# Prompt values of the expert layer by a dense pass over the value table, and another order of the row requests in the sample steps

## The reference

```
qh  = (xc @ wq) ...;  s = einsum(qh, sub_keys)          # 8 heads, two halves of 128 keys
sv, si = top_k(s, 16); cand = sv0[:, None] + sv1[None, :]; fv, fi = top_k(cand, 16)
eidx = si0 * 128 + si1 at fi;   g = softmax(fv)
act = gelu(einsum("td,trkd->trk", xc, u_tab[eidx]))
out = einsum("trk,trkd->td", g * act, v_tab[eidx])
h = h + out;   y = h + sigmoid(rmsnorm(h) @ w_gate) * (p @ w_ple)
```

## Time and profile before

| | |
|---|---|
| runs | 2516.59, 2518.28, 2526.69 us |
| profiled execution, span | 2524.0 us, 21534 instructions |
| PE busy | 1685.6 us (67%) |
| DVE busy | 1161.0 us (46%) |
| POOL busy | 913.2 us (36%) |
| ACT busy | 320.3 us (13%) |
| bytes moved by DMA | 908.75 MB, mean 360 GB/s |

### The profile page before, as it was taken

One profiled execution on the slowest core, in us unless ns is written; L12 is line 12 of the kernel. 1 busy time (PEld: TensorE's weight loads), 2 busy tenths in 40 slices (PEclk: granted clock), 3 DMA queues, 4 the chain that ended last, 5 costly groups with the idle time before them and its releaser, 6 DMA issues.

```text
span 2524.0 us, 21534 instructions
## 1 busy us (share of the span) xinstructions
PE 1685.6 (67%) x8372; PEld 917.0 (36%) x8372; DVE 1161.0 (46%) x2146; ACT 320.3 (13%) x705; POOL 913.2 (36%) x644
## 2 busy tenths in 40 slices
PE   8999989997997649688788332233333223577778
PEld 3445665696775337433376000000000000122224
DVE  2010322134455763544533666565565765644433
ACT  0000221010002322200200100101001012101002
POOL 0000000012234443422533556565666665645440
PEclk9998997998998776599699666656666665778799
DMA  9943483779999997999999999999999999999998
GB/s 358 333 164 123 125 315 107 268 254 411 366 399 375 369 379 301 391 382 373 400 411 360 418 418 422 421 421 421 422 421 421 421 421 418 402 416 416 416 415 325
DMA packets 215844, 908.75 MB, mean 360 GB/s; under 512 B 17350, under 2 KB 40879, under 8 KB 131808
## 3 DMA queue, kind: packets, MB, share of 16 engines
q0 software_dynamic: 92160, 671.13, 64.4%
q1 hardware_dynamic: 123126, 235.36, 26.3%
q10 hardware_dynamic: 458, 0.91, 0.1%
HBM read 895.31 MB, written 14.53 MB: 360 GB/s over the span
## 4 chain that ended last, share of the span: by engine, by line
DMA 48%; PE 40%; DVE 4%; POOL 3%; issue 3%; ACT 2%; SPq 0%; ACTq 0%; DVEq 0%; PEldq 0%; POOLq 0%
DMA arena<-in_peer_v,arena 31%; PE bank L1747 9%; PE bank L2182 5%; DMA arena<-in_w_in 5%; PE bank L2197 5%; DMA arena<-in_peer_u,arena 4%; DMA arena<-in_peer_wq 3%; DMA arena<-in_w_out 3%; PE bank L1821 3%; PE bank L1958 2%; PE bank L1934 2%; PE bank L2306 2%; PE bank L2131 2%; POOL arena L669 2%; PE bank L2108 1%
## 5 line engine op out<-in xcount | busy, mean ns | idle before, releaser
L1530 DVE CUSTOM_DVE_ANT_0 arena<-arena 128x2048 f32<-128x2048 f32 x320 | 730.7, 2292 | 581.5 <-DMA arena<-in_peer_u,arena 578.1
L2182 PE MATMUL bank<-arena 128*32 128x512 f32 x2560 | 459.9, 823 | 672.7 <-DVE arena L1539 539.1
L669 POOL DMA_INDIRECT arena<-in_peer_u,arena x320 | 561.2, 1754 | 860.6 <-DVEq L1509 566.4
L674 POOL DMA_INDIRECT arena<-in_peer_v,arena x320 | 351.7, 1099 | 689.6 <-PE bank L2182 663.2
L2182 PEld LDWEIGHTS bank<-arena 128*32 128x32 f32 x2560 | 67.1, 127 | 1003.7 <-DVE arena L1539 522.6
L1747 PE MATMUL bank<-arena 128*128 128x512 f32 (+2 forms) x544 | 216.3, 558 | 5.4 <-PE bank L1747 4.1
L2197 PE MATMUL bank<-arena 128*128 128x192 f32 x1024 | 189.9, 348 | 24.4 <-DMA arena<-in_w_in 23.2
L2197 PEld LDWEIGHTS bank<-arena 128*128 128x128 f32 x1024 | 181.5, 205 | 45.6 <-DMA arena<-in_w_in 28.5
L1747 PEld LDWEIGHTS bank<-arena 128*128 128x128 f32 (+1 forms) x544 | 101.4, 208 | 116.7 <-issue 116.4
L2306 PE MATMUL bank<-arena 128*128 128x512 f32 x256 | 125.6, 650 | 0.0
L986 ACT ACTIVATE arena<-arena 128x4 f32<-128x4 f32 x80 | 16.8, 210 | 849.6 <-DVE arena L1530 849.4
(11 more groups left out here) (270 smaller groups left out, 1490.5 us busy)
## 6 DMA issues: line engine op xcount, KB each, us to landing
arena<-in_w_in SPq DMA_DIRECT2D x22, 2048.0 KB, 9.4
arena<-in_w_in SPq DMA_DIRECT2D x32, 1024.0 KB, 14.6
arena<-in_w_out SPq DMA_DIRECT2D x8, 2048.0 KB, 9.7
arena<-in_peer_wq SPq DMA_DIRECT2D x8, 2048.0 KB, 8.1
arena<-in_w_out SPq DMA_DIRECT2D x16, 1024.0 KB, 16.3
arena<-in_peer_wq SPq DMA_DIRECT2D x16, 1024.0 KB, 23.0
arena<-in_ple_gate SPq DMA_DIRECT2D x32, 512.0 KB, 15.4
arena<-in_ple_gate SPq DMA_DIRECT2D x6, 2048.0 KB, 13.3
```

The source lines that it names most:

```text
L669: pool.indirect_dma_start(u_row[j], None, I["peer_u"][0], bass.IndirectOffsetOnAxis(idx[:, i, c + j:c + j + 1], 0)).then_inc(u_in[j], 16)
L674: pool.indirect_dma_start(v_row[j], None, I["peer_v"][0], bass.IndirectOffsetOnAxis(idx[:, i, c + j:c + j + 1], 0)).then_inc(v_in[j], 16)
L1530: dve.tensor_tensor_reduce(out=u_row[j], in0=u_row[j], in1=rep_of(i), scale=1.0, scalar=0.0, op0=ALU.mult, op1=ALU.add, accum_out=a4[:, pa ...
L2182: ins = pe.matmul(bank[i % 2][32 * q:32 * q + 32, :], diag[:, k % 2, j, :], v_row[j][:, 512 * q:512 * q + 512], start=(s == 0 and j == 0), ...
```

## The change

There are two parts.

For the eight prompt groups no value rows are gathered. After a group's dot products, its weights (32 tokens x 128 picks, one gelu for the whole group) are spread into a table of 128 x 128 experts per token: per step ScalarE builds four one-hot matrices of the first key index (`hot_rows`), VectorE four of the second, scaled by the weight (`hot_columns`), and TensorE multiplies them (`spread_picks`, four 128x128x128 matmuls); ScalarE copies the result (`spread_copy`) and writes it per group to DRAM (2 MB). The batches of a group run in the eight steps of the group behind it, those of the last group all in step 64. Then, in iterations 1 to 10 of the sample steps, TensorE multiplies the weights with the whole value table (134 MB, loaded by SyncE in 128 tiles of 1 MB): 32 `dense_group`s of 32 matmuls, 128x128 weights by 512 columns. VectorE adds each result to `h` (`dense_out`). The prompt's gate moves behind it, to iterations 11 to 14, eight quarters in each.

In the sample steps GpSimd no longer asks for four key tiles and then four value tiles: it asks for value tile j of step k and then key tile j of step k+1. In the prompt steps it asks for key tiles only.

Some semaphores are merged or renamed, and a row of 128 numbers is added to the constants; these edits are left out below.

```diff
+    BATCHES = 8 * DSUBS          # DSUBS = 8
+    GROUPS = 32
+    DENSE0, GATE0 = 1, 11
+    def groups_at(i, j):
+        n, slots = 4 * (i - DENSE0) + j, 4 * (GATE0 - DENSE0)
+        if not 0 <= n < slots:
+            return range(0)
+        return range(n * GROUPS // slots, (n + 1) * GROUPS // slots)
+    def batches_at(k):
+        if k < SSTEP or k > LAST:
+            return range(0)
+        return range(k - SSTEP, k - SSTEP + 1) if k < LAST else range(BATCHES - 8, BATCHES)
     # SyncE
+        def dense_rows(n):
+            c, half, pair = n // 8, n // 4 % 2, n % 4
+            if n >= 4:
+                sp.wait_ge(dense_used, n - 3)
+            j0 = 8 * c + 2 * pair
+            sp.dma_start(dense_v[n % 4], v_rows[:, j0:j0 + 2, 1024 * half:1024 * half + 1024]).then_inc(ring4_in[n % 4], 16)
+        sp.wait_ge(spread_out, 16 * (DSUBS - 1))
+        sp.wait_ge(spread_last, 16)
+        dense_weights(0)
+        for n in range(4 * GROUPS):
+            if n % 8 == 2 and n < 120:
+                dense_weights(n // 8 + 1)
+            dense_rows(n)
     # GpSimd
+        for k in range(LAST + 1):
+            for j in range(4):
+                key_rows(k, j)
+        for k in range(LAST, STEPS):
             for j in range(4):
+                value_rows(k, j)
+                if k + 1 < STEPS:
+                    key_rows(k + 1, j)
     # ScalarE
+        def hot_rows(n):
...
+            for x in range(4):
+                ins = act.activation(rows[:, x, :], key_iota, ACT.Square, scale=-1.0,
+                                     bias=pick_i[:, i % 4, t0 + x:t0 + x + 1])
+            ins.then_inc(squared, 1)
+            act.wait_ge(squared, n + 1)
+            act.activation(rows, rows, ACT.Relu, scale=-1.0, bias=1.0).then_inc(hot_i_ready, 1)
     # VectorE
+            for x in range(4):
+                ins = dve.tensor_scalar(hot_j[place][:, par, x, :], key_iota, pick_j[:, i % 4, t0 + x:t0 + x + 1],
+                                        wT[:, i % 2, t0 + x:t0 + x + 1], ALU.is_equal, ALU.mult)
+            ins.then_inc(hot_j_ready, 1)
+        def behind_dot(i, j):
+            if i == 0 and j == 0:
+                turn_weights(DSUBS - 1)
+                for n in batches_at(LAST):
+                    hot_columns(n)
+            for g in groups_at(i - 1, j):
+                dense_out(g)
     # TensorE
+        def dense_group(g):
+            c, half = divmod(g, 2)
+            if g == 0:
+                pe.wait_ge(spread_ev, BATCHES)
+            if half == 0:
+                pe.wait_ge(dense_set, 2 * c + 2)
+            for pair in range(4):
+                n = 4 * g + pair
+                pe.wait_ge(ring4_in[n % 4], dense_v_count(n))
+                for x in range(4):
+                    t, q = divmod(x, 2)
+                    if pair == 0 and 4 * g + x >= 6:
+                        pe.wait_ge(dense_ev, 4 * g + x - 5)
+                    for j in range(2):
+                        ins = pe.matmul(dense_bank(g, x)[:, :], dense_w[c % 2][:, 2 * pair + j, t].rearrange("p s t -> p (s t)"),
+                                        dense_v[n % 4][:, j, 512 * q:512 * q + 512],
+                                        start=(pair == 0 and j == 0), stop=(pair == 3 and j == 1))
+                    if pair == 3 and x < 3:
+                        ins.then_inc(dense_mm, 1)
+                ins.then_inc(dense_used, 1)
         for i in range(2 * SSTEP):
+            if i == GATE0:
+                h_turns()
...
+            for j in range(4):
+                for g in groups_at(i, j):
+                    dense_group(g)
+                weighted_tile(LAST + i, j)
+                if GATE0 <= i < GATE0 + 4:
+                    for q in range(2):
+                        prompt_gate(8 * (i - GATE0) + 2 * j + q)
```

More of the change, by code:

```diff
@@ L28 @@
 STEPS = SUBS * SSTEP
+DSUBS = 8
 EARLY = 4 * SSTEP
@@ L330, in ring_of, with dense_v_count, gate_count, dense_w_count @@
         return f % 3 if f < 16 else f % 4
+    def dense_v_count(n):
+        return 16 * (sum(ring_of(f) == n % 4 for f in range(32)) + n // 4 + 1)
+    def gate_count(q):
+        if q >= 29:
+            return 16 * 3
+        return 16 * ((11, 11, 10, 0, 0)[q % GW] + q // GW + 1)
+    def dense_w_count(c):
+        return 16 * (2 + c + 1)
     def ring_count(f):
@@ new lines, in spread_copy @@
+        def spread_copy(n):
+            i, t0 = n // 8, 4 * (n % 8)
+            act.wait_ge(spread_mm, n + 1)
+            if n % 8 == 0 and 0 < i < DSUBS - 1:
+                act.wait_ge(spread_out, 16 * i)
+            act.activation(spread[batch_place(n)[0]][:, :, t0:t0 + 4],
+                           batch_bank(n)[:, :].rearrange("p (t j) -> p j t", t=4), ACT.Copy).then_inc(spread_ev, 1)
+            if n % 8 == 7:
+                act.wait_ge(spread_ev, n + 1)
+                act.dma_start(w_dram[i], spread[batch_place(n)[0]].rearrange("p j t -> p (j t)"))                   .then_inc(spread_out if i < DSUBS - 1 else spread_last, 16)
@@ new lines, in step_batches, with dense_turn @@
+        def step_batches(k):
+            for n in batches_at(k):
+                hot_rows(n)
+                if n:
+                    spread_copy(n - 1)
+            if k == LAST:
+                spread_copy(BATCHES - 1)
+        def dense_turn(c):
+            if c >= 2:
+                act.wait_ge(dense_used, 8 * (c - 1))
+            for t in range(2):
+                act.wait_ge(half_in[t], dense_w_count(c))
+                act.activation(dense_w[c % 2][:, :, t], dense_in[t].rearrange("p s j t -> p j s t"), ACT.Copy).then_inc(dense_set, 1)
@@ L996, in acc_out @@
+        def acc_out(i):
+            act.wait_ge(v_used, 4 * SSTEP * (i - DSUBS + 1))
+            if i > DSUBS:
+                act.wait_ge(h_seen, 1)
             r = tile_of(i)[1]
@@ L1093, in _ @@
                     spread_rows(SUBS - 1, g)
-            if s == SSTEP - 1:
+            if k < LAST:
+                step_batches(k)
+            if k == LAST:
+                dense_turn(0)
+                dense_turn(1)
+            if k >= LAST and s == SSTEP - 1:
                 acc_out(k // SSTEP)
@@ L1506, in pick @@
             else:
+                if i < DSUBS:
+                    for turned, e in ((pick_i, e0), (pick_j, e1)):
+                        ins = dve.transpose(turned[:, i % 4, :], e.rearrange("p a b -> p (a b)"))
+                    step(ins)
                 step(dve.scalar_tensor_tensor(out=e0, in0=e0, scalar=float(NKEY), in1=e1, op0=ALU.mult, op1=ALU.add))
@@ L1662, in _ @@
                 spread_staged(i + 1)
-            if s == 0 and k:
+            if s == 0 and i > DSUBS:
                 add_peer(i - 1)
+            if s == 0 and 0 < i < DSUBS:
+                turn_weights(i - 1)
+            if k < LAST:
+                for n in batches_at(k):
+                    hot_columns(n)
             if k in late:
@@ L2242, in _, with spread_picks @@
             late_quarter(0, q)
+        def spread_picks(n):
+            place, par = batch_place(n)
+            pe.wait_ge(hot_i_ready, n + 1)
+            pe.wait_ge(hot_j_ready, n + 1)
+            if n >= 2:
+                pe.wait_ge(spread_ev, n - 1)
+            for x in range(4):
+                ins = pe.matmul(batch_bank(n)[:, NKEY * x:NKEY * x + NKEY], hot_i[place][:, par, x, :], hot_j[place][:, par, x, :],
+                                start=True, stop=True)
+            ins.then_inc(spread_mm, 1)
         for k in range(EARLY):
```

327 lines of the change are left out of this document (189 added, 138 removed).

## The result

The changed kernel takes 2993.55 us (median of four runs, 2984.87 to 2997.2) against 2519.61 us (the median with a fourth run): the ratio is 1.187, with a 95% interval of 1.184 to 1.191. The forecast was 2920 us, a ratio of 1.16, and a range of 2830 to 3050. The direction and the main mechanism were right.

A forecast was written before the change was run, and what follows sets the result against it. DMA bytes were taken to bound most of the kernel, with TensorE idle time. From step 0 at 560 us, 638 + 465 + 41 + 975 + 198 + 40 gave about 2920 us; range 2830 to 3050.

The forecast's parts named there:

- What bounds the kernel, and where the pass stands: Bytes are scarce and TensorE has idle time, but the dense pass stands behind step 64, none in steps 28 to 63.
- The pass, 975 us: Iterations 1 to 10: 1024 matmuls at 0.873 us, 894; tiles 45, group boundaries 20, empty slots and clock dips 16.
- Steps 0 to 27, 638 us: Now 824 us, less 132.8 of value tiles' TensorE work and 53.0 of idle time; ends 521 and 752.
- I let these be paid by the waits that shrink: Steps 0 to 27: added picks (TensorE 24 us) and batch work cost nothing net, as waits shrink with DMA load.
- keep their chain: Rival, 12%: in the first 28 steps one wait takes another's place, 752 us instead of 638, 3035 in all.
- Steps 28 to 63, 465 us: Now 732 us; VectorE takes over from DMA at 12.75 us a step, 459, plus 6 for short steps.
- The lock rival: Rival, 8%: in prompt steps each dot also waits for GpSimd's issue, 16.4 us a step, 3045 in all.
- Step 64, 41 us: Step 64 until the pass: batches 22, last copy 1, write 7, weight load back 4, turning and dot 0; ends 25, 60.
- The order of the requests, 0 us: Sample steps: GpSimd's alternating value and key tiles move nothing, at most a tile's 6 us of landing.
- The rival on bytes: Rival, 3%: 100 MB less moved decides, 2473 us at 0.437 us a dense matmul; gain below 0.486.
- The signs: Step 28 near 1200, step 64 near 1660, 12 to 13 us a step between, VectorE above 90% busy, DMA near 0.8.
- the three signs of being wrong: A dense matmul under 0.8 us, TensorE waiting for table tiles, or steps 28 to 63 at 15 us or more.

The follow-up runs named there:

- experiments 3 to 5: Changed kernel with half the dense matmuls left out, with only the first four table tiles loaded, and with both: 2637.8, 2993.2 and 2555.0 us.
- 6: Changed kernel with 12 of 32 dense groups skipped and 384 matmuls of the same shape on constants put into steps 32 to 63: 2746.5 us.
- 10: Changed kernel with batches 2 to 23 (steps 10 to 31) left out on ScalarE, VectorE and TensorE: 2985.8 us.
- 9: Changed kernel without VectorE's one-hot matrices in steps 10 to 63: 2970.6 us.
- 1 and 2: Changed kernel with the old request order in the sample steps, 2998.37 us; kernel before with only the new order there, 2527.47 against 2526.31 us.

## Why the prediction was right, and which terms were off

*What bounds the kernel, and where the pass stands*: right, and shown from both sides. The pass is TensorE's alone (experiments 3 to 5), in a place where it lies beside nothing it could hide in, while in the 413 us of steps 33 to 63 TensorE could take 304 us of matmuls, without their table tiles, for nothing (6).

*The sum*: nearer than its terms. It was 123 us short up to the pass and 52 too large from there on. That these cancel in part is luck.

*The pass, 975 us*: 930. The price of a matmul was exact, 0.869 for 0.873. What I added was too much: the 36 us for group boundaries, empty slots and clock dips were 4.4 us of idle time, and the clock was 1.00 in the mean; the tiles were 41 us for 45. The 930 lie at the lower end that was given, and under the 950 to 1000 named as a sign.

*Steps 0 to 27, 638 us*: 676, and by the better mark, step 33, 76 us late (1338.5 for 1262). The step that failed is "I let these be paid by the waits that shrink". Of the 186 us taken out, 148 were gained. The picks took TensorE 28 us, near the 24 forecast, but it also waits 39.8 us for ScalarE's squares, since its list puts them between two blocks of other work. That wait is not the whole cause: with it gone, weights come late instead (10). The rival "keep their chain" named this mechanism, one wait in another's place, at its full size, 752 us, 114 over the forecast; a third of that happened by step 28 and two thirds by step 33. Steps 28 to 32 took 99.7 us for five: VectorE is busy 67 us of them, and waits 15.1 us for TensorE's picks behind its last query block and 13.1 for key rows.

*Steps 28 to 63, 465 us*: 515. About 35 us of the 50 stand in steps 28 to 32, which is the early chain's end. In steps 33 to 63 it is 13.4 us for 12.9, waits for key rows and ScalarE (9). The lock rival, 16.4 us, did not happen. GpSimd's issues that start within a dot take 2.2 us (median) and end 0.8 us behind it, those that start outside take 0.94; the 320 dots take 2.28 to 2.36 us, and 23 of them that start while an issue of the second kind runs take 2.28 to 2.31. The Trainium skill's "SBUF — State Buffer", section "SBUF: two separate sides", has whichever of the two starts first hold the shared pair while the other fully blocks; the trace agrees where VectorE comes first, and does not where GpSimd does.

*Step 64, 41 us*: 76. The batches took the 22 us forecast; mis-sized was the weight load back, 4 us forecast and 25.3 measured, and missing were ScalarE's four copies (7.7 us, part of them beside the write) and the turn of the second weight tile ahead of a gelu (13.6 us). The 76 lie outside the ends given, 25 and 60. I had followed the arithmetic and not the order of ScalarE's list.

*The order of the requests, 0 us*: right, as far as 1 and 2 can tell, to some 5 us.

*Iterations 11 to 15, 198, and the tail, 40*: 191 and 40.

*The rival on bytes*: its turning point, 0.486 us a matmul, was wrong. At half the matmuls the kernel still takes 2638 us, because the pass and the sample gathers share DMA and here take 579 us. Their 228 MB (394 GB/s x 579 us) would take 543 at 420 GB/s and the kernel near 2602, an estimate, so with the table loaded behind step 64 no cheaper matmul makes this change pay. Even with half of the matmuls and no table at all it takes 2555.

*The Trainium skill's "TensorE: Matmul & The Clock Gate"*, section "Back-to-back issue gap": its sustained spacing, times the four passes, gave the prediction's estimate of 2560 us. The trace disagrees, 0.869 us a matmul for 0.52.

*The signs*: step 28 came 39 us and step 64 91 us late. Steps of 12 to 13 us came out at 14.3, 13.4 from step 33 on, with VectorE 89% and then 94% busy. The DMA share, 0.81, the 2048 records and the 245 GB/s beside the pass are as named. None of the three signs of being wrong was seen.

## What to carry to other kernels

Trading bytes for matmuls pays here only if the matmuls can stand where the engine idles, and their operands' bytes with them: read from the order of the lists where they must stand, and price both there. Count the records of the same shape for the price; it was right to 0.5%, while the term argued from "other waits will pay for this" was 38 us too small. When one resource is relieved, look for the second floor before naming a turning point.

## What the runs showed that was not expected

The first two loads of 0.5 MB, in pieces of 1 KB, landed 15.1 and 25.3 us after their issue, while GpSimd's queue moved 9.3 MB of gathers; over the kernel their median is 7.8 us, and 5.8 us for a table tile of 1 MB. TensorE held a granted clock of 1.00 (0.98 in its lowest 100 us) through 930 us at full load, and 0.96 in steps whose clock was 0.50 when it had little to do.
